# Value stage of a two-group decoder layer: gates read for eight key blocks at a time, split activations four deep

## The reference, cut to what matters

```
def run_block(args):
    t, g, e = args
    act = jax.nn.gelu(jnp.einsum('nd,nhkd->nhk', t, u_tab[e]), approximate=False)
    return jnp.einsum('nhk,nhkd->nd', g * act, v_tab[e])
```

## Time and profile before

| | |
|---|---|
| runs | 2214.03, 2215.4, 2217.62 us; median 2215.4 |
| span of the profiled execution | 2214.2 us (the page names no other time for it) |
| busy share PE, DVE, ACT, POOL | 93%, 69%, 33%, 37% |
| DMA | 683.00 MB in 202351 packets, mean 308 GB/s |
| value stage | about 1600 to 2195 us |

### The profile page before, as it was taken

How to read it: one execution, slowest core, us unless ns; L and a number is a source line. 1 busy time by engine, 2 the same in 40 slices (tenths; PEclk the granted TensorE clock), 3 DMA queues, 4 the chain that set the end, 5 groups by cost and what they waited for, 6 DMA issues and landing times.

```text
span 2214.2 us, 34004 instructions
## 1 busy us (share of the span) xinstructions
PE 2065.0 (93%) x12186; PEld 1717.4 (78%) x12186; DVE 1522.6 (69%) x3144; ACT 737.6 (33%) x1111; POOL 824.7 (37%) x497
## 2 busy tenths in 40 slices
PE   7999989999888979999999999999898899999896
PEld 7999975555442439999999999999787777777775
DVE  1384135564752330188988989999798898989798
ACT  2232124343420011234333346655333333333232
POOL 4333300001200004357877851112543565556550
PEclk9999999999978999999999999999999999999998
DMA  9998987885786667359976977788999999999993
GB/s 329 357 319 317 338 340 303 313 322 191 248 323 227 249 247 284 114 206 341 337 259 216 300 252 282 276 301 323 393 394 393 383 395 392 393 384 392 368 393 145
DMA packets 202351, 683.00 MB, mean 308 GB/s; under 512 B 18305, under 2 KB 84225, under 8 KB 194177
## 3 DMA queue, kind: packets, MB, share of 16 engines
q1 hardware_dynamic: 150832, 439.29, 54.8%
q0 software_dynamic: 46080, 167.79, 20.0%
q10 hardware_dynamic: 5328, 74.52, 9.4%
HBM read 618.78 MB, written 196.32 MB: 368 GB/s over the span
## 4 chain that ended last, share of the span: by engine, by line
PE 45%; DMA 21%; DVE 16%; issue 11%; POOL 4%; ACT 3%; SPq 0%; DVEq 0%; POOLq 0%; ACTq 0%
DMA overlay<-peer_v 13%; PE bank L188 9%; PE bank L189 9%; PE bank L190 9%; PE bank L1426 5%; DMA overlay<-peer_u 5%; POOL overlay L1579 3%; DVE arena L2025 3%; DVE overlay L2208 2%; PE bank L644 2%; PE bank L628 2%; PE bank L694 1%; PE bank L667 1%; DVE arena L1800 1%; DMA arena<-peer_rows,arena 1%
## 5 line engine op out<-in xcount | busy, mean ns | idle before, releaser
L188 PE MATMUL bank<-overlay 128*128 128x384 f32 (+4 forms) x2832 | 964.6, 341 | 76.5 <-DVE overlay L2212 53.0
L189 PE MATMUL bank<-overlay 128*128 128x384 f32 (+4 forms) x2832 | 950.3, 336 | 0.0
L190 PE MATMUL bank<-overlay 128*128 128x384 f32 (+4 forms) x2832 | 949.6, 335 | 0.0
L188 PEld LDWEIGHTS bank<-overlay 128*128 128x128 f32 (+1 forms) x2832 | 536.7, 190 | 124.8 <-issue 83.2
L189 PEld LDWEIGHTS bank<-overlay 128*128 128x128 f32 (+1 forms) x2832 | 536.9, 190 | 30.9
L190 PEld LDWEIGHTS bank<-overlay 128*128 128x128 f32 (+1 forms) x2832 | 535.4, 189 | 32.4
L1579 POOL TENSOR_TENSOR overlay<-overlay 128x1024 fp32r<-128x1024 f32 x98 | 251.2, 2571 | 319.9 <-ACT overlay L1572 319.1
L1845 POOL DMA_INDIRECT arena<-peer_v,arena x160 | 254.2, 1588 | 181.5 <-DVE arena L2025 166.9
L1845 POOL DMA_INDIRECT arena<-peer_rows,arena x112 | 137.2, 1225 | 293.5 <-DVE arena L2020 279.9
L2025 DVE SCALAR_TENSOR_TENSOR arena<-arena 128x1024 f32<-128x1024 f32 x160 | 204.2, 1276 | 0.1
L2121 ACT CAST overlay<-overlay 128x1024 fp32r<-128x1024 f32 x128 | 134.2, 1048 | 147.0 <-DMA overlay<-peer_v 130.9
(11 more groups left out here) (236 smaller groups left out, 2094.4 us busy)
## 6 DMA issues: line engine op xcount, KB each, us to landing
overlay<-peer_u SPq DMA_DIRECT2D x128, 512.0 KB, 6.7
overlay<-peer_v SPq DMA_DIRECT2D x128, 512.0 KB, 12.0
o_ks<-cache_k ACTq DMA_DIRECT2D x11, 4088.0 KB, 17.6
o_vsall<-cache_vall SPq DMA_DIRECT2D x21, 2044.0 KB, 12.3
arena<-cache_kT SPq DMA_DIRECT2D x32, 896.0 KB, 11.1
arena<-cache_v SPq DMA_DIRECT2D x56, 512.0 KB, 6.5
arena<-w_out SPq DMA_DIRECT2D x48, 512.0 KB, 5.6
act<-arena SPq DMA_DIRECT2D x128, 192.0 KB, 7.1
```

The costliest lines, as they stand in the source:

```text
L188: pe.matmul(out, lhs[0], rhs[0], start=start, stop=False)
L189: pe.matmul(out, lhs[0], rhs[1], start=False, stop=False)
L190: return pe.matmul(out, lhs[1], rhs[0], start=False, stop=stop)
```

## The change

The gates are loaded once a pair of groups, for eight blocks, in 128 x 12 runs of 8 x 128 = 1024 bytes, 1.5 MB each, into one of two buffers of twice the size (`ggrp`, at 26 and 62 of the arena). The load for pair x + 1 is issued in the second group of pair x, behind that group's gelus. The first load, ahead of the stage, now brings blocks 0 to 7. To free the room, the ring `ga` of split activations is four deep, at 50 and 56, and ACT waits before L2125 until PE is done with block a - 4. `vs` stays eight deep. SP's loop goes over two pairs at a time, so that the buffer's number is fixed in the code.

```diff
-        ga = overlay(50, 8, DEN, kind=F32R), overlay(62, 8, DEN, kind=F32R)
+        ga = overlay(50, 4, DEN, kind=F32R), overlay(56, 4, DEN, kind=F32R)
-        ggrp = [cut(at, GRP * DEN) for at in (26, 32)]
+        ggrp = [cut(at, 8 * DEN) for at in (26, 62)]
...
-        def sp_gates(sp, x, par):
-            g = x * 2 + par
-            sp.dma_start(ggrp[par].rearrange("p (s a n) -> p s (a n)", a=GRP, n=SLAB),
-                         t["gate"].rearrange("s p a n -> p s (a n)")[:, :, bass.ds(g * (GRP * SLAB), GRP * SLAB)])\
-                .then_inc(gate_in[par], 16)
+        def sp_gates(sp, x, odd):
+            sp.dma_start(ggrp[odd].rearrange("p (s a n) -> p s (a n)", a=8, n=SLAB),
+                         t["gate"].rearrange("s p a n -> p s (a n)")[:, :, bass.ds(x * (8 * SLAB), 8 * SLAB)])\
+                .then_inc(gate_in[odd], 16)
...
-            def group(x, par):
+            def group(x, par, odd, more=True):
                 sp_gelus(sp, x, par)
-                sp_gates(sp, x, par)
+                if par == 1 and more:
+                    sp_gates(sp, x + 1, 1 - odd)
                 for k in range(GRP):
                     sp_rows(sp, x, par, k)
 
-            group(0, 1)
-            with sp.Fori(1, PAIRS) as x:
-                for par in range(2):
-                    group(x, par)
+            group(0, 1, 0)
+            with sp.Fori(0, PAIRS // 2 - 1) as y:
+                for odd in (1, 0):
+                    for par in range(2):
+                        group(y * 2 + (2 - odd), par, odd)
+            for par in range(2):
+                group(PAIRS - 1, par, 1, False)
...
+                    act.wait_ge(vp_done, x * 8 + (j + 5))
                     act.wait_ge(weighted, x * 8 + (j + 9))
-                    act.copy(ga[0][:, j], prod[j % 2]).then_inc(ga_hi, 1)
+                    act.copy(ga[0][:, j % 4], prod[j % 2]).then_inc(ga_hi, 1)
...
-                            mm = product(pe, bank[:, 2 * i + half, :], [w[:, j, i * P:(i + 1) * P] for w in ga],
+                            mm = product(pe, bank[:, 2 * i + half, :], [w[:, j % 4, i * P:(i + 1) * P] for w in ga],
...
-                    dve.wait_ge(gate_in[par], 16 * (a // 8 + 1))
+                if j == 0:
+                    dve.wait_ge(gate_in[a // 8 % 2], 16 * (a // 16 + 1))
...
-                                  ggrp[par].rearrange("p (s a n) -> p s a n", a=GRP, n=SLAB)[:, :, k], ALU.mult).then_inc(weighted, 1)
+                                  ggrp[a // 8 % 2].rearrange("p (s a n) -> p s a n", a=8, n=SLAB)[:, :, j], ALU.mult).then_inc(weighted, 1)
...
-                dve.tensor_tensor(ga[1][:, j], prod[j % 2], ga[0][:, j].bitcast(F32), ALU.subtract).then_inc(ga_lo, 1)
+                dve.tensor_tensor(ga[1][:, j % 4], prod[j % 2], ga[0][:, j % 4].bitcast(F32), ALU.subtract).then_inc(ga_lo, 1)
```

## The result

The changed kernel takes 2232.05 us as a median of 15 runs (2219.63 to 2252.61), the kernel before 2217.62 in its 15 (2210.74 to 2229.32). The medians are 14.4 us apart; the ratio taken over the runs of both is 1.0052, with a 95% interval of 1.0027 to 1.0077. So the change makes the kernel slower by some 11 us (6 to 17), where 2205 and faster was forecast and 2219 was the upper end of the range. The profiled execution has a span of 2233.5 us, 19.3 more than the profiled one of before; its run (2235.57 us) is the twelfth of the 15, so its trace tells where time went, and the ratio how much.

The account below looks back on a forecast made before the run. DMA, 98% full, was taken to bound the value stage: 548.6 + 11.0 + 5 = 564.6 us, 11.4 less than 576. With 1 us for the U loads, 2214.2 - 10.4 + 1.2 = 2205 us; range 2196 to 2219.

Parts of the forecast that it names:

- DMA is 98% full: Value stage: DMA is the bound, with 9040 of 9216 us of engine time as work and 11.0 us idle.
- 24,576 packets go, x 9.5 ns ... 14.6 us: Value stage gates: fewer packets at 9.5 ns each save 233 us of engine time, 14.6 us of the stage.
- 1.8 us: Value stage bytes: 0.786 MB more is loaded ahead of the stage, which takes 1.8 us of DMA work out of it.
- 3.5 ns a packet: DMA packet price estimated from the skill page, 5.4 us for 24,576 packets; the forecast used the measured 9.5 ns instead.
- The loss is between 0 ... and 15 x 0.7 = 10.5 us. I take 5: Value stage: idle DMA time added by alternating groups with and without gates, up to 0.7 us a group; 5 us taken.
- the slower rival: Value stage: value rows wait behind larger gate bursts; -3 to +24 us, middle +10, 2226 us; chance 0.13.
- delayed by more than 2.0 us: Value stage: bursts decide if a group with gates is delayed over 2.0 us and DMA then idles in the light group.
- DVE idle over 60 us: Value stage: with DMA's share under 1.0 in most light groups, the sign that bursts decide and the forecast is wrong.
- A stall of 1.0 to 2.8 us: Ahead of the value stage: the larger first gate load delays U's load and stalls PE; 1 us taken.
- A late gate transfer costs nothing by itself: Value stage, block 44: value rows behind the gates are later still, so nothing is counted for gates coming earlier.
- ga four deep ... Cost 0: Value stage: the shorter split-activation ring and ACT's new wait for PE cost 0, upper bound 1 us.
- The median to be added to: Whole kernel: the median of three timed runs, 2215.4 us, is 1.2 above the span, so 1.2 was added.

Follow-up runs that it names:

- e1: The kernel before with only the ring of split activations cut to four deep, with ACT's new wait; 1.0015 of the kernel before.
- e3: The changed kernel with each eight-block gate load split by slabs into two 0.75 MB halves, one a group; 0.9992 of the kernel before.
- e5: The changed kernel with gate loads halved by slabs, one half a group, and the first load cut to blocks 0 to 3; 0.9958, 2207.06 us.
- e10: The changed kernel with gates in four three-slab transfers between value rows, and a first load of blocks 0 to 3; 0.9958, 2208.01 us.
- e8_deep_bursts: The changed kernel with a ring of eight for raw value rows, issued a group ahead, split rows four deep; 0.9976 of the kernel before.

## Why the prediction was wrong

- "DMA is 98% full", the bound: right. The count of packets in flight in the kernel before falls short by 4.1 us in 576. The eight other stages with even bursts or a longer lead (e1, e3 and e5 to e10) are 12 to 17 us above their DMA work.
- "24,576 packets go, x 9.5 ns ... 14.6 us" and "1.8 us": right. Forecast work 548.6, measured 548.0. The halves, with bursts of 0.75 MB as before and 1 KB runs, turn it into a stage 13 us shorter. The estimate of 3.5 ns a packet from the Trainium skill (DMA: Bandwidth & Descriptors, Why small descriptors are slow) is less than half of what the rows say, and the 512 B for line rate that the Trainium skill gives (same page, Specifications) don't agree with this trace: 332 GB/s with 512-byte packets, 416 without.
- "The loss is between 0 ... and 15 x 0.7 = 10.5 us. I take 5": **this step failed**. It was 26 us (37.0 against 11.0); packets in flight alone show 12 of them (16.1 against 4.1). The bound counted what a light group, one without gates, needs (15.6 us) against DVE's pace (16.3), as if DMA entered it with its usual backlog or exactly none. It enters ahead: a group with gates makes DVE stand 5.2 us on average (73.3 / 14), in that time the gather's ring fills, and what was fetched early is missing as work in the group without. The longer lead (e8_deep_bursts) and the even bursts (e3_halves) each took most of the loss away. The condition for the slower rival stood in the prediction, "delayed by more than 2.0 us", with 3.6 us as its delay at half the engines; that was above 2.0, and still I gave it 0.13. Its time, 2226, is the nearest to the measured one (1.0052 x 2217.62 = 2229), in part by luck: it is the middle between -3 and +24 and holds nothing for the start, which cost 6. The sign that was named for it, "DVE idle over 60 us", could not tell much, since DVE stood 60.8 us before.
- "A stall of 1.0 to 2.8 us", taken as 1: too small, the second term that failed. The load of U came 5.2 us later than its 13.9; PE stood 4.3 us, and the stage began about 6 us later (6 to 8.5 in the five traces with that load). A share of all or half the engines for the added 0.786 MB (1.8 to 3.6 us) doesn't give 5.2; why the load drains more slowly is open.
- "A late gate transfer costs nothing by itself": right. L2204's 22.5 us of waits are gone, and nothing was gained by it: the waits for value rows are longer.
- "ga four deep ... Cost 0": right, by the ring alone. ACT waited for PE once, 3.0 us.
- The median to be added to was taken from three runs. 15 runs of the same kernel spread over 18.6 us, and it was 2.2 us higher: small beside the error.

In the profiled execution the 26 us of idle time less 17 of work make the stage's 9. They and the 6 us ahead of it, with the profiled run's own 2 and 2 us, make 19.3. What the smaller first load gains on top of the halves, 0.34 points or 7.5 us, fits the table (start 8.5 shorter, stage 1.6 longer), but the intervals are nearly as wide.

## What to carry to other kernels

When DMA is the bound, split its time into work (packets by a price each, bytes by a price each) and idle time, and forecast both: a cheaper transfer gains only what the order of the queue lets it. Before merging loads, compare the longest run of bytes ahead of the tile that is waited for with that tile's lead; if it is longer, cut the merged load across its other dimension, so that the run length grows and the burst doesn't. Here that turned a loss of 0.5% into no change (0.9992), and with the first load left at its old size as well into a gain of 0.4% (e5_halves_first, 2207.06 us; the quarters have the same ratio).

## What the hardware showed unexpectedly

A burst of 3072 packets of 512 bytes costs more than its own work: against 1536 packets of 1 KB with the same bytes, 13.5 us of work in the stage by the price became 29 us of time (614 against 585).

The profile's DMA share depends on packet size. These are windows of the kernel before (columns as in the earlier trace rows), the two stretches of the first pair in the earlier trace rows, the one with 512-byte packets first:

```profile
1844.00:1848.00 4.00, 4.00 (x11) 3.13 (x10) 4.00 (x6) 1.46 (x2) 2.69 (x3) 0.52 1.12 332
1840.00:1844.00 4.00, 0.60 (x2) 0.51 (x3) 3.62 (x4) 1.81 (x3) 0.93 (x1) 0.63 1.04 416
```

The share is 1.12 and 1.04, though both are full by the sum of packets and bytes (the prices come in part from these two rows, but their fit to all full stretches says the same). So a fall from 1.04 to 1.01 says nothing about idle time (11.0 us before, 17.3 with halves).
